# The last 2048 of 16384 experts computed for all tokens at once, the others gathered with an index bound; 64x64 products for the weighted sum

## What is computed

```
q = (x @ w_query).reshape(B, T, 8, 2, 128)          # 8 heads, two half queries
s1, s2 = q[..., 0, :] @ sub_keys_1.T, q[..., 1, :] @ sub_keys_2.T     # 128 keys each
v1, i1 = top_k(s1, 16);  v2, i2 = top_k(s2, 16)
top_s, top_pos = top_k(v1[..., :, None] + v2[..., None, :], 16)       # of 256 sums
experts = take(i1 * 128 + i2, top_pos)              # 16 of 16384 for each token and head
g = softmax(top_s)
hdn = gelu(expert_down[experts] . x)                # one number for each choice
y = sum(g * hdn * expert_up[experts])               # rows of 1024 numbers
out = rms_norm(h + y, norm_f_g)
```

## Time and profile before

| | |
|---|---|
| median of 3 runs | 945.86 us (944.13 to 947.71) |
| span of the profiled execution | 862.9 us |
| time of the profiled execution | not listed apart; median less span is 83.0 us |
| PE, DVE, ACT, POOL busy | 88%, 65%, 21%, 67% of the span |
| granted TensorE clock | 0.998 |
| bytes | 308.39 MB, 268.47 of them by the gathers |

### The profile page before, as it was taken

The page is one execution under the profiler, slowest core; times in us unless marked ns, Lnnn a source line. Parts: engine busy times, 40 slices in busy tenths (PEclk is TensorE's granted clock), DMA queues, the critical chain, the costliest instruction groups (busy, mean ns, idle before and its releaser), DMA issues.

```text
span 862.9 us, 9305 instructions
## 1 busy us (share of the span) xinstructions
PE 755.6 (88%) x2473; PEld 390.9 (45%) x2473; DVE 564.1 (65%) x1503; ACT 180.2 (21%) x563; POOL 575.1 (67%) x716
## 2 busy tenths in 40 slices
PE   9999999999999879788888888888879797777786
PEld 6988668556554424244333434343434242222232
DVE  3565686239999667676767676666676666765445
ACT  2134455211212021122202030202020202112021
POOL 6886451017767777777777777777777777777770
PEclk9999999999999999999999999999999999999999
DMA  8948450659999999999999999999999999999997
GB/s 304 232 133 243 156 236 5 242 243 363 409 380 410 409 409 409 410 409 410 409 409 410 410 410 409 410 409 409 410 410 410 409 410 409 410 410 410 409 409 292
DMA packets 99487, 308.39 MB, mean 357 GB/s; under 512 B 18504, under 2 KB 23424, under 8 KB 99456
## 3 DMA queue, kind: packets, MB, share of 16 engines
q0 software_dynamic: 73728, 268.47, 78.3%
q1 hardware_dynamic: 24656, 39.39, 13.8%
q10 hardware_dynamic: 1072, 0.16, 0.1%
HBM read 306.41 MB, written 1.05 MB: 356 GB/s over the span
## 4 chain that ended last, share of the span: by engine, by line
PE 27%; DMA 27%; POOL 24%; issue 12%; DVE 8%; ACT 1%; DVEq 0%; ACTq 0%
PE bank L1530 24%; POOL region_w L647 18%; DMA region_w<-in_expert_up,chosen 14%; DMA region_w<-in_expert_down,chosen 11%; POOL gates L647 3%; DMA pool_bd<-in_expert_down,chosen 2%; PE xn_ps L1530 2%; PE bank L1533 2%; DVE region_w L1392 1%; POOL dn_spare L647 1%; POOL pool_bd L647 1%; DMA dn_spare<-in_expert_down,chosen 1%; DVE gates L1392 1%; DVE pool_bd L1392 1%; DVE region_q L1166 0%
## 5 line engine op out<-in xcount | busy, mean ns | idle before, releaser
L1530 PE MATMUL bank<-region_w,pool_bd 128*128 128x512 f32 (+2 forms) x1006 | 473.1, 598 | 96.6 <-DMA region_w<-in_expert_up,chosen 89.2
L1530 PEld LDWEIGHTS bank<-region_w,pool_bd 128*128 128x128 f32 x1006 | 174.4, 189 | 366.4 <-issue 294.5
L647 POOL DMA_INDIRECT region_w<-in_expert_up,chosen x250 | 234.8, 939 | 82.7 <-issue 61.4
L1392 DVE CUSTOM_DVE_ANT_0 region_w<-xn_ps,region_w 128x1024 f32<-128x1024 f32 x128 | 156.6, 1224 | 101.4 <-DMA region_w<-in_expert_down,chosen 101.0
L647 POOL DMA_INDIRECT region_w<-in_expert_down,chosen x128 | 120.6, 943 | 40.8 <-issue 32.9
L1392 DVE CUSTOM_DVE_ANT_0 gates<-xn_ps,gates 128x1024 f32<-128x1024 f32 x64 | 78.1, 1223 | 36.7 <-DMA gates<-in_expert_down,chosen 33.1
L908 ACT ACTIVATE pool_bd<-ident,pool_bd 128x128 f32<-128x128 f32 x251 | 78.4, 389 | 77.2 <-PE bank L1530 53.8
L647 POOL DMA_INDIRECT gates<-in_expert_down,chosen x64 | 60.4, 943 | 23.4 <-issue 16.5
L711 ACT ACTIVATE pool_bd<-bank 128x256 f32<-128x256 f32 (+3 forms) x49 | 19.0, 389 | 265.5 <-PE bank L1530 241.3
L1530 PE MATMUL bank<-region_q,oT 128*128 (+1 forms) x240 | 54.3, 379 | 0.0
L1392 DVE CUSTOM_DVE_ANT_0 dn_spare<-xn_ps,dn_spare 128x1024 f32<-128x1024 f32 x32 | 39.2, 1224 | 18.8 <-DMA dn_spare<-in_expert_down,chosen 18.6
(11 more groups left out here) (289 smaller groups left out, 786.8 us busy)
## 6 DMA issues: line engine op xcount, KB each, us to landing
region_q<-in_w_in SPq DMA_DIRECT2D x4, 2048.0 KB, 8.4
region_q<-in_w_query SPq DMA_DIRECT2D x1, 6144.0 KB, 23.9
region_w<-in_expert_up,chosen POOLq DMA_INDIRECT x250, 13.9
region_w<-in_w_out SPq DMA_DIRECT2D x1, 3072.0 KB, 20.9
x_sb<-in_x SPq DMA_DIRECT2D x4, 512.0 KB, 4.0
region_q<-in_w_in SPq DMA_DIRECT2D x2, 1024.0 KB, 11.4
region_q<-in_w_in SPq DMA_DIRECT2D x16, 128.0 KB, 3.0
region_w<-in_wb_nsa SPq DMA_DIRECT2D x2, 1024.0 KB, 16.6
```

What stands on the lines that cost most here:

```text
L647: pool.indirect_dma_start(out=row, out_offset=None, in_=table, in_offset=bass.IndirectOffsetOnAxis(ap=of_slot(chosen, s, k), axis=0)).then ...
L1392: dve.tensor_tensor_reduce(out=row, in0=xn_ps[:, :], in1=row, scale=1.0, scalar=0.0, op0=ALU.mult, op1=ALU.add, accum_out=hdn[:, k:k + 1]) ...
L1530: return pe.matmul(out_, lhsT, rhs, start=start, stop=stop)
```

## The change

- The first key's last 16 values, experts 14336 to 16383, are **left out of the gathers**: `indirect_dma_start` gets `bounds_check=LOW_ROWS - 1, oob_is_err=False`. Of such a choice no row is copied, its buffer keeps what it held, and its coefficient is multiplied by zero (`keep`).
- These 2048 experts are **computed for all 256 tokens**: SP loads their down rows in 16 blocks of 128; PE turns each (`turn_down`, 8 transposes) and multiplies it with the normed tokens (`hidden`, 8 products of 256 columns); ACT copies, and makes the gelu of two blocks at once (`dense_gelu`). The weights of the softmax are spread on a grid of tokens by 2048 experts: DVE makes one-hot rows (`hot_columns`), PE one product of 16 columns for each token (`grid`), DVE multiplies with the gelu (`weigh_dense`). SP loads the 16 blocks of up rows and PE adds them (`add_dense`, for each tile one full product and two of 64 output rows).
- **Weighing** a row is four products of 64x64 by 512 columns in place of two of 128x128; the second bank of a tile holds its two halves of tokens exchanged. Diagonals are 128x64.
- **Queries** 2 to 15 are made transposed (`ask`: 16 products of 128 columns), so that the two transposes and one of two copies go. They are asked and chosen earlier, at fixed rows (`ASK_AT`, `KEYS_AT`).
- The loops of DVE and PE are written out; where each piece of dense work stands between the rows is fixed by tables (`TURN_AT`, `HIDDEN_AT`, `TABLE_AT`, `GRID_AT`, `UP_AT`). Up rows use the 8 buffers of `ring_up` to the end, DVE adds no rows, and the residual is put into PSUM first (`start_sum`). The final sum of squares crosses the exchanged halves by small products (`token_sums`).

```diff
+DENSE = 16
+LOW_KEYS = NK - DENSE
+LOW_ROWS = LOW_KEYS * NK
+GTOK = 32
+NGROUPS = TOK // GTOK
+ASK_AT = {1: 3, 4: 4, 7: 5, 10: 6, 13: 7}
+ASK_AT.update({29 + 4 * i: 8 + i for i in range(NH)})
+KEYS_AT = {3: 3, 9: 4}
+KEYS_AT.update({17 + 9 * i: 4 + i for i in range(1, 12)})
+TURN_AT = {62 + 4 * j: j for j in range(DENSE)}
+HIDDEN_AT = {64 + 4 * j: j for j in range(DENSE)}
+TABLE_AT = {68: 0, 130: 1}
+GRID_AT = {140 + (15 * g) // 2: g for g in range(NGROUPS)}
+UP_AT = {198 + (17 * j) // 5: j for j in range(DENSE)}
+ACT_LEAD = 6
+PACE_CHOICE, PACE_HOT = 1.9, 1.6
...
# SP
+            sp.wait_ge(q_mm, STEPS + 2)
+            for j in range(DENSE):
+                if j >= 2:
+                    sp.wait_ge(turned_mm, j - 1)
+                sp.dma_start(raw_d[j % 2], a["expert_down"][LOW_ROWS + j * P:LOW_ROWS + (j + 1) * P, :]).then_inc(dense_in[j % 2], 16)
+            for j in range(DENSE):
...
+                    sp.wait_ge(dense_used, j - 3)
+                sp.dma_start(u_rows[j % 4], a["expert_up"][LOW_ROWS + j * P:LOW_ROWS + (j + 1) * P, :]).then_inc(dense_in[j % 4], 16)
...
# POOL
                 pool.indirect_dma_start(
                     out=row, out_offset=None, in_=table,
-                    in_offset=bass.IndirectOffsetOnAxis(ap=of_slot(chosen, s, k), axis=0)).then_inc(arrived, 16)
+                    in_offset=bass.IndirectOffsetOnAxis(ap=of_slot(chosen, s, k), axis=0),
+                    bounds_check=LOW_ROWS - 1, oob_is_err=False).then_inc(arrived, 16)
...
-                if n == 4 * SLOTS:
+                if n == 2 * SLOTS:
                     rstd_h(1)
-                if n == LAST * SLOTS:
-                    pool.wait_ge(ssq3, 1)
-                    rstd(stat[:, 26:27], stat[:, 24:25], DM).then_inc(rstd3, 1)
...
# DVE
-                link(dve.tensor_copy(dots, hdn))
+                link(dve.tensor_tensor(out=dots, in0=hdn, in1=of_step(keep, s), op=ALU.mult))
...
+            def hot_columns(g):
+                r, first = g % 2, GTOK * g
...
+                own.mark(dve.tensor_tensor(out=one_a[r], in0=bc(tab[:, 0, first:first + 1], [[1, GTOK], [0, DENSE]]),
+                                           in1=bc(iota128[:, LOW_KEYS:LOW_KEYS + 1], [[0, GTOK], [1, DENSE]]), op=ALU.is_equal))
...
+                for n in range(0, GTOK, 4):
+                    dve.tensor_tensor(out=one_b[r][:, n:n + 4, :], in0=bc(tab[:, 1, first + n:first + n + 1], [[1, 4], [0, P]]),
+                                      in1=bc(iota128[:, 0:1], [[0, 4], [1, P]]), op=ALU.is_equal).then_inc(hot_ready, 1)
...
# PE
+            def ask(p):
...
+                for half in range(2):
+                    at_ = head * 256 + half * P
+                    for k in range(KC):
+                        last = mm(banks[6][:, half * P:(half + 1) * P], wq[:, k, at_:at_ + P], oTv[:, k, tok_rows[t]], k == 0, k == KC - 1)
...
+            def weigh(n):
+                s, k = n // SLOTS, n % SLOTS
+                t = tile_of(s)
+                pe.wait_ge(diag_ready, n + 1)
+                pe.wait_ge(up_in[n % RING], 16 * (n // RING + 1))
+                row = ring_up[:, n % RING, :]
+                end = n == NROWS - 1
+                for r, rows in enumerate(HALF64):
+                    mm(banks[2 * t][rows, :], diag[rows, k, :], row[rows, cols[0]], False, end)
+                    last = mm(banks[2 * t + 1][HALF64[1 - r], :], diag[rows, k, :], row[rows, cols[1]], False, end)
+                last.then_inc(up_used, 1)
...
+            def grid(g):
...
+                for n in range(GTOK):
+                    last = mm(banks[6][:, DENSE * n:DENSE * (n + 1)], one_b[g % 2][:, n, :], one_a[g % 2][:, n, :])
...
+            def add_dense(j):
...
+                for t in range(2):
+                    first = t * P
+                    end = t == 0 and j == DENSE - 1
+                    mm(banks[2 * t][:, :], hw[:, j, first:first + P], u_rows[j % 4][:, cols[0]], False, end)
+                    for rows, part in zip(HALF64, (first + 64, first)):
+                        last = mm(banks[2 * t + 1][rows, :], hw[:, j, part:part + 64], u_rows[j % 4][:, cols[1]], False, end)
+                last.then_inc(dense_used, 1)
```

More of the change, by code:

```diff
@@ new lines, in choices, with dense_weights @@
+            def choices():
+                for n, p in KEYS_AT.items():
+                    if p > 3:
+                        yield from not_before(n + 18)
+                        yield from choose(p, tile_of(p))
+                yield from not_before(n + 28)
+                normalise(LAST)
+                own.wait()
+                dve.engine_nop().then_inc(keys_read, 1)
+                yield
+            def dense_weights():
+                yield from hot_columns(0)
+                yield from hot_columns(1)
+                for n, g in GRID_AT.items():
+                    yield from not_before(n + 18)
+                    yield from weigh_dense(g)
+                    if g + 2 < NGROUPS:
+                        yield from hot_columns(g + 2)
@@ L1492, in _ @@
[L1492 to L1498 removed]
+                    if s == 3 and 8 <= k < 12:
+                        next(scaled)
+                    if s == 2 and k < SLOTS - AHEAD:
+                        continue
+                    credit += PACE_HOT if chosen_all else PACE_CHOICE
@@ new lines, in _ @@
+            dve.wait_ge(up_used, NROWS)
+            halves = [one_b[r][:, 0:4, :].rearrange("p a b -> p (a b)") for r in range(2)]
+            link(dve.tensor_copy(halves[0], banks[3][:, :]))
+            dve.tensor_tensor_reduce(out=halves[1], in0=halves[0], in1=halves[0], scale=1.0 / DM, scalar=0.0,
+                                     op0=ALU.mult, op1=ALU.add, accum_out=half_sum(1, 1)).then_inc(ssq2, 1)
+            dve.tensor_tensor(out=xs[:, 1, cols[1]], in0=halves[0], in1=gfb[:, cols[1]], op=ALU.mult).then_inc(out_ready, 1)
@@ L1989, in _ @@
-            for half in range(2):
-                for k in range(4):
-                    last = mm(banks[2 + half][:, k * P:(k + 1) * P], bc(ident[0:KC, 4 * half + k:4 * half + k + 1], [[0, P]]), gf_nat)
-                last.then_inc(gain_mm, 1)
-            with pe.Fori(1, 4) as i:
-                step_turn(0, i, ask=0, ahead=-1)
-            pe.wait_ge(gain_held, 3)
-            for half in range(2):
-                hiddenT(1, half)
-            back(1, back_mm)
-            with pe.Fori(4, NH) as i:
-                step_turn(0, i, ask=1, ahead=-1)
@@ L2001, in _ @@
-            weigh(SLOTS - 1, NH - 1, stop=(0, 1))
-            weigh(0, NH, start=True)
-            with pe.Fori(NH, NH + 4) as i:
-                step_turn(1, i, ask=1, ahead=1)
-            with pe.Fori(NH + 4, LAST - 1) as i:
-                step_turn(1, i, ahead=1)
-            for k in range(1, SLOTS):
-                weigh(k, LAST - 1)
-            for nth, k in enumerate(WEIGHED):
-                weigh(k, LAST, stop=(1,) if k == WEIGHED[-1] else (), nth=nth)
-            pe.wait_ge(added, 1)
```

553 lines of the change are left out of this document (305 added, 248 removed).

## The result

The changed kernel takes **1066.67 us** (median of 4 runs, 1057.83 to 1075.31), the kernel before 946.79 beside it; the ratio is 1.120, 95% interval 1.110 to 1.129. The forecast was 934 with a range of 903 to 982: wrong in sign, and outside.

What follows compares the result with a forecast made beforehand. Two chains were taken to bound the kernel, bytes (656 us) and gather issue (635). First gather 192.2 + issue 634.7 + waits 10 + landing 6 + tail 8.0 = 850.9, plus 83.0 outside the span: 934 us, range 903 to 982.

Steps and rivals of the forecast that it cites:

- waits 10: POOL's waits between first and last gather: 10 us, 4.2 early, the rest for PE's tight stretches.
- Bytes: Gathers on q0: skipped rows take out 38.9 MB, dense loads return 16.8; net 22.1 MB, 54 us at 409 GB/s.
- Rival 5: Gathers: a skipped row still moves, 285.2 MB, last landing 41 us later: 988 us; 4%.
- rival 1: Gathers: the bytes decide, because a gather with skips is cheaper: 908 us, 894 without PE's part; 12%.
- Rival 2: Gathers: skips fall unevenly over the DMA engines, the fullest 5 to 6% over the mean: 942 us; 15%.
- Issue of gathers: POOL: still 512 gathers, 1.242 us apart, unchanged by the bound; 511 intervals stay 634.7 us.
- rival 3: POOL: the bound makes each gather dearer, deciding from 0.023 us on; +0.05 is 960, +0.1 is 985; 20%.
- PE, the grid at 256 x 2 x 0.10 = 52: PE's grid of weights: 256 products of two passes at 0.10 us each, 52 us in all.
- a clock below full in the weighing rows: PE's weighing: a sign of being wrong, excluded because PE's gaps per row stay near 1.3 us.
- rival 4: PE's weighing: four tiles don't overlap, only pairs, 2.0 us a row: about 1060 us; 7%.
- from row 198 on 7.9 against 8.45: Last stretch, per 3.4 rows: PE needs 7.9 us against POOL's 8.45, close but not the bound.
- 83.0 us outside the span unchanged: Before's 945.86 median less its 862.9 span, taken as time outside the span and added to the forecast span.

Runs made afterwards that it cites:

- the best variant: Changed kernel with grid taken up at n + 26, choices at n + 22, hidden products five rows behind transposes, choice 2's exponentials before the gain copy: 915.92 us, 1.058.
- both kernels made for it: Kernel before with the query's transposes six rows behind it, or its eight products spread over rows 2 to 5: 865.10 and 865.30 us beside 864.79.

## Why the prediction was wrong

In the terms of its sum, with the 964.0 us span of the 865 chip against the forecast 850.9: the first gather is 0.5 later; the issue of 511 gathers is 662 and not 634.7, 27 more; the waits between gathers are 88 and not 10, 78 more; and from the last gather to the end are 21.1 and not 14.0, 7 more. The step that failed is the term "waits 10". One by one:

1. **Bytes** (rows that are left out don't move, q0 near 230 MB): right, 229.65. Rival 5 is out, and rival 1 too, since the DMA engines have slack. Rival 2, the uneven skips, got no run of its own; without the dense loads nothing of it is seen, since gathers 100 to 450 are 1.302 us apart there, near the 1.295 of issue alone. Beside the dense loads it stays open.
2. **Issue of gathers** ("I take no change"): wrong. The bound adds 0.053 to 0.056 us to each; rival 3's mechanism is true, near the +0.05 it worked out first. Times 511 it is 27 us against the 12 of the forecast gain. The Trainium skill (DMA: Bandwidth & Descriptors, Anatomy of one DMA) calls descriptor generation small; the traces disagree for gathers, 0.937 busy each and 0.993 with a bound. It was not the largest loss, and the run without the bound, 19 us slower, shows that under the dense loads the bytes repay it.
3. **PE, the grid at 256 x 2 x 0.10 = 52**: mis-sized. The passes took 0.19 on the mean, 97 us in all. The clock is nearly the whole of it: bursts of 64 took 12.7 us at a clock of 0.55 and 10.5 at 0.68 in the changed kernel, 8.7 at 0.83 in the best variant, and length times clock is 7.0 to 7.2 us each time, 0.11 a pass. The sentence that failed is the one that excluded "a clock below full in the weighing rows" since the gaps stay near 1.3 us: there were gaps (0.8 us a row in the variant without dense path and bound), and the clock fell all the same, to 0.69 in rows with nothing but weighing. The prediction had priced every pass by rows at 2.4 GHz. The weighing itself, at 1.09 alone and 0.92 in a run (3.66 us for four rows) at that clock, was sized well, 285 us busy in all where it had 294, and rival 4 is out; the Trainium skill (TensorEngine Tiling (Array Packing), Key Properties) says that the four tiles run independently, and the traces agree.
4. **"Waits 10"**: the step that failed most. The sums of PE, DVE and ACT each lay under POOL's and did so in the trace (PE 87 of 100 at worst), but the waits of one for another were set at 10 us with no row behind them. By POOL's order (SLOTS + LAG) VectorE runs about 21 rows ahead of TensorE, and the change makes it wait, in order, for a burst behind TensorE's row n once it is at its own row n + 18, three rows too early: 86 us of VectorE, 45 of the kernel, shown by changing the one number. `normalise(2)` behind the gain copy: 12 us of gathers, over half of it given back by moving one operation. The hidden products two rows behind the transposes: 7. The prediction did say what is behind a waiting instruction on POOL and ACT, and not for VectorE's wait for the grid.
5. **The tail and the last gathers**: "from row 198 on 7.9 against 8.45" left TensorE no room. The last 62 gathers take 94.6 us against 80.5, and 80.3 without the dense path, so it is the dense up rows. The change also drops `up_place`, which let the last up rows land in the down rows' places; with the bound and no dense path that costs nothing. In the variant without the bound as well they take 89.5; there `up_place` may be the cause, which no run shows. Behind the last gather TensorE still has a dense block and six rows to add, and the end comes 21.1 us after it instead of 6 + 8.0.
6. **"83.0 us outside the span unchanged"**: wrong, 1.7 to 2.2. It would have moved the number and not the sign.

By the steps, on 865 chips (changed less before, 109 us): order of the grid 45, two other waits of order 12, together 57; the remaining 51 of the best variant are, by its gathers, 8 of dearer issue in the 150 gathers from the 100th, 18 from 250 to 450 where TensorE is full (11 of them issue), 16 in the last 62, where the dense up rows stand, and 10 from 53 to 100, less 2 of tail. The first 57 are measured by moving the waits; the shares of the 51 are read from the times of the gathers and no run takes them apart.

Open: what makes a chip slow. On the 945 chips engines start late behind one another once the gathers run, and gathers stand 1.44 us apart at 0.937 busy; no run settled whether the late starts behind a query cost the time or only fill it, since both kernels made for it ran on 865 chips. Slower memory isn't ruled out either: a 4 KB packet of the gathers took 173 ns on the mean there, and 164 on the page of before.

## What to carry to other kernels

Sums of busy time by engine say whether work fits, not whether its order does. For every wait that a change adds, write down how many rows ahead the waiting engine runs of the one it waits for, and put the wait behind that distance. Passes priced from a dense stretch hold only at that clock; where a change makes TensorE's work smaller or narrower, price them at the 1.2 GHz level too. And compare span with time for each run on its own chip before any difference between them is called overhead.

## What the runs showed of the hardware

- Four 64x64 tiles of fp32 with 512 columns overlap: eight passes 1.09 us alone and 0.92 in a run, against 1.95 for two full products; at 1.2 GHz 1.98. The granted clock falls with them: 0.69 with TensorE busy 67 of 100 us, where the kernel before with its full products keeps 1.00 at 83; on one 945 chip 0.80 with four tiles and 0.95 with full products. In the variant without dense path and bound gathers 100 to 450 took only 1.5 us longer for it, with the 1.98 below the 2.48 of two gathers.
- A pass of 16 columns with 128x128 weights took 0.198 us at a clock of 0.55 and 0.135 at 0.83, with the weight loads busy throughout. That is 0.11 us at the full clock, what a pass of 128 columns takes in the earlier trace rows; so here the load rather than the columns seems to set the price, at either clock.
- A bound on an indirect gather of 128 rows costs 0.056 us more of POOL, 993 against 937 ns (median), and the shortest of 256, at 987 ns, is not cheaper by its skips. A skipped row is still a packet: q0 keeps its 73,728, and 9,486 more of them than before (2 x 4,743) have 4 bytes and take 9 ns, where a 4 KB one takes 164 to 178 on the mean.
- Chips of one type differ by 9% on the same program, steadily. The engines' busy times differ by 0 to 2% (TensorE 771 against 756 us at a clock of 0.94, VectorE 564 on both) and a gather's 937 ns not at all; most of the 81 us between the two spans is waiting.
